# RWKV-7 preparation in a one-layer hybrid encoder: a denser triangular substitution, moved bonus, and moved elementwise work

## The reference, cut to what matters

```python
w_log = -softplus(-(w0 + tanh(w_l) @ w2)) - 0.5
decay = exp(-exp(w_log)); a = sigmoid(a0 + a_l @ a2); g = sigmoid(g_l) @ g2
kk = heads(k * k_k); kk = kk / max(sqrt(sum(kk * kk)), 1e-12)
k = k * (1 + (a - 1) * k_a)
state = state * w + (state @ -kk) (kk * a)^T + v k^T     # token by token
y = state @ r
y = groupnorm(y) * ln_w + ln_b + sum(r * k * r_k) * v    # the bonus
out = y * g
```

## Time and profile before

| what | value |
|---|---|
| median of 3 runs | 1804.3 us (1803.42 to 1804.86) |
| the profiled execution, its own time | 1807.21 us |
| its span, first to last instruction | 1805.4 us |
| PE busy | 1738.3 us (96%) |
| DVE / ACT / POOL busy | 988.2 / 796.3 / 693.3 us |
| mean granted TensorE clock | 0.979 |

### The profile page before, as it was taken

The page is one execution under the profiler, slowest core; times in us unless marked ns, Lnnn a source line. Parts: engine busy times, 40 slices in busy tenths (PEclk is TensorE's granted clock), DMA queues, the critical chain, the costliest instruction groups (busy, mean ns, idle before and its releaser), DMA issues.

```text
span 1805.4 us, 30026 instructions
## 1 busy us (share of the span) xinstructions
PE 1738.3 (96%) x11960; PEld 1321.0 (73%) x11960; DVE 988.2 (55%) x1551; ACT 796.3 (44%) x1519; POOL 693.3 (38%) x502
## 2 busy tenths in 40 slices
PE   7999999999998998999999999999999999999997
PEld 4766666665575766768888768878888888888886
DVE  6543232325464756453340462388856775884788
ACT  5313233235342443541120232467666666756763
POOL 2211202010120111223333103398686876968772
PEclk9999999998989999999999999999999999999999
DMA  5101000000212114051211102202202022030202
GB/s 206 47 24 33 22 35 13 21 5 18 54 20 43 26 40 110 27 205 38 79 47 49 33 0 65 75 25 70 77 29 83 24 70 66 28 93 25 70 1 93
DMA packets 81681, 94.36 MB, mean 52 GB/s; under 512 B 53648, under 2 KB 56208, under 8 KB 81552
## 3 DMA queue, kind: packets, MB, share of 16 engines
q1 hardware_dynamic: 81552, 92.56, 16.7%
HBM read 82.57 MB, written 9.98 MB: 51 GB/s over the span
## 4 chain that ended last, share of the span: by engine, by line
PE 85%; DVE 7%; DMA 3%; ACT 3%; issue 2%; POOL 1%; SPq 1%; DVEq 0%; ACTq 0%; POOLq 0%
PE PS L1652 33%; PE PS L934 16%; PE PS L994 8%; PE PS L1095 3%; PE PS L1113 2%; PE PS L1134 2%; PE PS L1599 2%; PE PS L1168 1%; PE PS L1577 1%; PE PS L1444 1%; PE PS L1459 1%; DMA xt_dram<-sc_s 1%; PE PS L1171 1%; PE PS L1359 1%; PE PS L1302 1%
## 5 line engine op out<-in xcount | busy, mean ns | idle before, releaser
L1652 PE MATMUL PS<-memr,wsp 128*128 128x512 f32 x1332 | 319.9, 391 | 2.4 <-POOL wsp L895 2.4
L934 PE MATMUL PS<-xn,wsp 128*128 128x512 f32 x1344 | 309.1, 391 | 6.7 <-DVE xn L2212 6.7
L934 PEld LDWEIGHTS PS<-xn,wsp 128*128 128x128 f32 x1344 | 252.8, 189 | 62.8 <-DVE xn L2212 5.9
L1652 PEld LDWEIGHTS PS<-memr,wsp 128*128 128x128 f32 x1332 | 249.7, 188 | 57.7 <-POOL wsp L895 3.3
L776 POOL CAST wsp<-wraw 128x1024 fp32r<-128x1024 f32 x40 | 42.7, 1068 | 468.8 <-PE PS L934 302.3
L1652 PE MATMUL PS<-memr,wraw_r 128*128 128x512 f32 x684 | 165.7, 391 | 0.7 <-POOL wraw_r L895 0.7
L994 PE MATMUL PS<-xn,wsp 128*128 128x512 f32 x576 | 149.5, 407 | 3.3 <-DVE proj L2261 3.1
L895 POOL TENSOR_TENSOR wsp<-sa,wsp 128x512 fp32r<-128x512 f32 x86 | 115.2, 1342 | 89.9 <-ACT wsp L2103 89.8
L1652 PEld LDWEIGHTS PS<-memr,wraw_r 128*128 128x128 f32 x684 | 128.2, 188 | 29.1 <-POOL wraw_r L895 1.1
L994 PEld LDWEIGHTS PS<-xn,wsp 128*128 128x128 f32 x576 | 106.4, 192 | 41.4 <-issue 20.7
L1776 ACT ACTIVATE H<-PS,mst 128x128 f32<-128x128 f32 (+3 forms) x64 | 47.5, 743 | 184.9 <-DVE mst L2342 179.7
(11 more groups left out here) (349 smaller groups left out, 3170.3 us busy)
## 6 DMA issues: line engine op xcount, KB each, us to landing
wraw<-in_weights_dram SPq DMA_DIRECT2D x40, 512.0 KB, 3.6
sa<-in_weights_dram SPq DMA_DIRECT2D x32, 512.0 KB, 4.2
H<-in_x_dram SPq DMA_DIRECT2D x16, 512.0 KB, 6.7
sbx<-in_weights_dram SPq DMA_DIRECT2D x32, 256.0 KB, 2.9
sa<-in_weights_dram SPq DMA_DIRECT2D x32, 256.0 KB, 2.8
H<-in_weights_dram SPq DMA_DIRECT2D x8, 512.0 KB, 6.5
out_dram<-sbx SPq DMA_DIRECT2D x16, 256.0 KB, 2.1
a_dram<-H SPq DMA_DIRECT2D x16, 128.0 KB, 2.5
```

The source lines that it names most:

```text
L934: last = nc.tensor.matmul(PS[:, 2 * k + half, :], wsp[:, k, kt, a, :], src[:, at, b, HALF * half:HALF * half + HALF], start=(i == 0 and (a ...
L1652: last = nc.tensor.matmul(PS[:, g % PS_BANKS, :], w[:, a, win(k)], x[:, b, :], start=(k == 0 and (a, b) == (0, 0)), stop=(k == ROWS - 1 an ...
```

## The change

- **Substitution**: steps j = 8 to 14 move from places 29 to 33 to places 28 to 30, `xt` from 33 to 30. The bonus moves from places 31 and 32 to 33 and 34.
- **Moves between engines**: `kk` (the scaled key) goes from VectorE to ScalarE (place 9, a copy with a scale), and ScalarE squares the unscaled key with the scale inside the activation (place 4). `na` goes to ScalarE (place 3). `b` goes to GpSimd (place 13).
- **Order**: `ks0`, `ks1` one place sooner (5, 6); `kf` at 7, `W` and `Wi` at 8; `nkk` at 12, `k2` at 13, `rt` at 14; the `al` products one place sooner (17 to 20); `rk` at 22; memsets at 23. The table for heads 6 and 7 follows.
- **One activation table**: explicit loads of a set that holds both logarithm and exponential, at the start, before the latent norms and at place 6. A dummy logarithm at the start goes.
- **`local`**: the two products with a selection matrix per head (L1359) both use all 128 rows. Before, one of them used 64 rows.
- **Ahead of the loop**: places 0 to 3 of pair 1 run before the doubling of pair 0, not between its steps, on TensorE and VectorE.
- **SyncE**: a wait on `tok` of the pair before is added ahead of one load.

```diff
-SUBST = {26: (0, 1, 2, 3), 27: (4, 5, 6, 7), 29: (8,), 30: (9,), 31: (10, 11), 32: (12, 13), 33: (14,)}
-BONUS = 31
+SUBST = {26: (0, 1, 2, 3), 27: (4, 5, 6, 7), 28: (8, 9, 10, 11), 29: (12, 13), 30: (14,)}
+BONUS = 33
...
-                return ((0,), (1,), (2,), (3, 4), (5, 6), (7, 8, 9), (10, 11), (12, 13, 14), (15, 16, 17))[i]
-            return ((), (18, 19), (20, 21, 22), (24,), (), (26, 27), (29, 30, 31), (32, 33), ())[i - 9]
+                return ((0,), (1,), (2,), (3, 4), (5, 6), (7, 8, 9), (10, 11), (12, 13), (14, 15, 16))[i]
+            return ((), (17, 18), (19, 20), (21, 22, 23), (), (26, 27), (28, 29, 30), (33, 34), ())[i - 9]
...
                 if p < PAIRS - 1:
+                    if p >= 1:
+                        sp.wait_ge(L_PE.sem, L_PE.at(f"tok{p - 1}_{NW - 1}", -1))
                     sp.dma_start(o_places[p], o_dram[p]).then_inc(o_loaded, 16)
...
+                if s == 13:
+                    pool.wait_ge(P_DVE.sem, P_DVE.at(f"nkk_{n}", -1))
+                    nc.gpsimd.tensor_tensor(rA, rA, rKK, ALU.mult).then_inc(P_POOL.sem, P_POOL.one(f"b_{n}"))
...
-                    for c, rows in ((h, chunk(h)), (1 - h, slice(0, P))):
-                        last = nc.tensor.matmul(to_r(c), con[rows, C_SEL + CH * h:C_SEL + CH * h + CH],
-                                                rAR[p % 2][rows, w, 1, chunk(c)], start=False, stop=True)
+                    for c in range(2):
+                        last = nc.tensor.matmul(to_r(c), con[:, C_SEL + CH * h:C_SEL + CH * h + CH],
+                                                rAR[p % 2][:, w, 1, chunk(c)], start=False, stop=True)
...
+            for s in range(4):
+                beside(0, s)
             for lv in range(LEVELS):
                 for w in range(2):
                     double_q(lv, 0, w)
-                beside(0, 2 * lv)
                 for w in range(2):
                     double_z(lv, 0, w)
-                beside(0, 2 * lv + 1)
...
+            nc.scalar.preload_act_table_set("natural_log_exp_and_others")
             for kt in range(KT):
                 act.wait_ge(x_loaded[kt], 16)
...
             act.wait_ge(eps_made, 1)
-            nc.scalar.activation(small[:, 41:42], small[:, 40:41], ACT.Ln)
...
+                if s == 3:
+                    r_at(P_ACT, f"ta1_{n}")
+                    nc.scalar.activation(rA, rA, ACT.Copy, scale=-0.5, bias=-0.5).then_inc(sem_, one("na"))
+                if s == 4:
                     if n >= 2:
                         r_at(L_PE, f"tok{n - 2}_{NW - 1}")
-                    nc.scalar.activation(rBh[i], rKK, ACT.Square).then_inc(sem_, one("kksq"))
+                    nc.scalar.activation(rBh[i], proj[:, T_K + n, :], ACT.Square, scale=vech[:, 8 + n:9 + n]).then_inc(
+                        sem_, one("kksq"))
+                if s == 6:
+                    nc.scalar.preload_act_table_set("natural_log_exp_and_others")
...
-                if s == 33:
+                if s == max(SUBST):
                     own(f"xa{BLK - 2}")
                     r(nc.vector.tensor_copy(bXT, bX.rearrange("p i n -> p n i")), "xt")
```

More of the change, by code:

```diff
@@ L477, in build @@
                                            "rk0", "rk1"]))
-        P_ACT = Steps(sem("prep_act"), each(["tw0", "tw1", "ta0", "ta1", "kksq", "kl0", "kl1", "W", "kf", "Wi", "wt0", "wt1", "afirst"]))
+        P_ACT = Steps(sem("prep_act"), each(["tw0", "tw1", "ta0", "ta1", "na", "kksq", "kl0", "kl1", "kf", "W", "Wi", "kk", "wt0", "wt1", "afirst"]))
         P_DVE = Steps(sem("prep_dve"), each(
[L480 to L483, removed]
+            ["t1p", "L", "am", "nkk", "k2", "at", "bt", "kt", "al0", "al1", "al2", "al3", "rk", "x0", "x1"]
+            + [y for place in SUBST for j in SUBST[place] for y in (f"xm{j}", f"xa{j}")] + ["xt", "bv0", "bv1"]))
+        P_POOL = Steps(sem("prep_pool"), each(["b", "rt", "kh", "bh"]))
         O_PE = Steps(sem("post_pe"), each(["vs0", "vs1", "lg0", "lg1"]))
@@ L1831, in prep @@
                     nc.scalar.activation(rB[i][:, halves(s - 6)], PS[:, 7, :], ACT.Ln).then_inc(sem_, one(f"kl{s - 6}"))
-                if s == 10:
+                if s == 7:
+                    r_at(P_ACT, f"kl1_{n}")
+                    nc.scalar.activation(rB[i], rB[i], ACT.Exp, scale=-0.5).then_inc(sem_, one("kf"))
+                if s == 8:
                     r_at(P_DVE, f"L_{n}")
@@ L1837, in prep @@
                     nc.scalar.activation(rW, rWi, ACT.Exp, scale=-half_e).then_inc(sem_, one("W"))
-                    r_at(P_ACT, f"kl1_{n}")
-                    nc.scalar.activation(rB[i], rB[i], ACT.Exp, scale=-0.5).then_inc(sem_, one("kf"))
-                if s == 11:
                     r_at(P_ACT, f"W_{n}")
                     nc.scalar.activation(rWi, rWi, ACT.Exp, scale=half_e).then_inc(sem_, one("Wi"))
-                if s == 12:
+                if s == 9:
+                    nc.scalar.activation(rKK, proj[:, T_K + n, :], ACT.Copy, scale=vech[:, 8 + n:9 + n]).then_inc(
+                        sem_, one("kk"))
+                if s == 10:
                     if n >= 2:
@@ L2400, in prep @@
                     r(nc.vector.tensor_tensor_scan(rWi, rStep, rT1, 0.0, ALU.mult, ALU.add), "L")
-                if s == 4:
-                    r_at(P_ACT, f"ta1_{n}")
-                    r(nc.vector.tensor_scalar(rA, rA, -0.5, -0.5, ALU.mult, ALU.add), "na")
-                if s == 4:
-                    own("na")
+                if s == 5:
+                    r_at(P_ACT, f"na_{n}")
+                    own("L")
                     r(nc.vector.tensor_scalar(rT1, rA, 1.0, vec[:, V_KA + n:V_KA + n + 1], ALU.add, ALU.mult), "am")
-                if s == 5:
+                if s == 12:
+                    r_at(P_ACT, f"kk_{n}")
+                    r(nc.vector.scalar_tensor_tensor(rKK, rB[i], 1e12, rKK, ALU.min, ALU.mult), "nkk")
+                if s == 13:
                     own("am")
                     r(nc.vector.scalar_tensor_tensor(rT1, rT1, 1.0, kk_, ALU.subtract, ALU.mult, reverse0=True), "k2")
-                if s == 14:
-                    r_at(P_ACT, f"kf_{n}")
-                    r(nc.vector.scalar_tensor_tensor(rKK, rB[i], 1e12, rKK, ALU.min, ALU.mult), "nkk")
                 if s == 15:
@@ L2421, in prep @@
                 if s == 16:
-                    r(nc.vector.tensor_tensor(rA, rA, rKK, ALU.mult), "b")
-                if s == 16:
-                    own("b")
+                    r_at(P_POOL, f"b_{n}")
                     r_at(P_ACT, f"Wi_{n}")
@@ L2429, in prep @@
                     r(nc.vector.tensor_tensor(kk_, rT1, rWi, ALU.mult), "kt")
-                if 18 <= s < 22:
-                    k = s - 18
+                if 17 <= s < 21:
+                    k = s - 17
                     r_at(P_PE, f"al{k}_{n}")
@@ L2440, in prep @@
                         f"al{k}")
-                if s == 21:
+                if s == 22:
                     r_at(P_POOL, f"rt_{n}")
                     r(nc.vector.scalar_tensor_tensor(r_, r_, vec[:, V_RK + n:V_RK + n + 1], rT1, ALU.mult, ALU.mult), "rk")
-                if s == 24:
+                if s == 23:
                     if n >= 1:
@@ L2449, in prep @@
                     r(nc.vector.memset(sc_s[:, 3456:3712:BLK + 1], 1.0), "x1")
-                if s in (BONUS, BONUS + 1):
-                    k = s - BONUS
-                    r_at(P_PE, f"rk{k}_{n}")
-                    if k == 0 and n == 0:
-                        m_at(M_PE, f"qp{MLA_HEADS - 1}")
-                    r(nc.vector.tensor_tensor(rBV[n][:, halves(k)], PS[:, 7, :], v_[:, halves(k)], ALU.mult), f"bv{k}")
                 if s in SUBST:
@@ L2468, in prep @@
                         r(nc.vector.tensor_tensor(below, below, part, ALU.add), f"xa{j}")
-                if s == 33:
+                if s == max(SUBST):
                     own(f"xa{BLK - 2}")
                     r(nc.vector.tensor_copy(bXT, bX.rearrange("p i n -> p n i")), "xt")
+                if s in (BONUS, BONUS + 1):
+                    k = s - BONUS
+                    r_at(P_PE, f"rk{k}_{n}")
+                    if k == 0 and n == 0:
+                        m_at(M_PE, f"qp{MLA_HEADS - 1}")
+                    r(nc.vector.tensor_tensor(rBV[n][:, halves(k)], PS[:, 7, :], v_[:, halves(k)], ALU.mult), f"bv{k}")
             def post(m, s):
```

26 lines of the change are left out of this document (9 added, 17 removed).

## The result

The changed kernel is slower: 1827.0 us median of 4 runs (1823.1 to 1827.7) beside 1803.9 of 4 for the kernel before. The ratio on record is 1.0141, with a 95% interval of 1.0119 to 1.0163; the quotient of the two medians, 1.0128, lies inside it. Two executions in the chip's slow state (2800.65 us of the kernel before, 1938.71 us of the one with five things undone) are in no ratio here. I had predicted 1806, range 1797 to 1812. The profiled execution after took 1823.12 us over a span of 1821.3, 15.9 more than the span of before; the other three spans were 1824.8 to 1825.9.

A forecast was written before the change was run, and what follows sets the result against it. TensorE, busy 96% of the span, was taken as the bound, with room only in the RWKV loop. Gains and costs summed to +1.6 us on an expected median of 1804.3, rounded to 1806 us; range 1797 to 1812.

The forecast's parts named there:

- `b` on GpSimd: In the preparation, b takes 2.4 us on GpSimd and ends before bt reads it: nothing; 0.5 a pair if nkk were late.
- The stalls: TensorE's three waits for inverse matrices from DRAM vanish because xt ends 3.9 us sooner: -7.6 us.
- The clock behind them: After those DRAM waits, the low granted clock costs 2.5, 1.4 and 1.4 us, which come back: -5.3 us.
- The denser order's own waits: In group 2, TensorE waits for VectorE's state copy and scores, partly offset by mt coming sooner: +1.05 us.
- Tables: Activation table loads removed at the start (-1.3 us) and in pair 3 (-0.75 us); nothing in post or the latent norms.
- Head 6: TensorE's 2.25 us standstill before ks0, from late squares on ScalarE, shrinks: -1.7 us (nothing to -3.5).
- `al0` in the gap of `mt`: In group 1, al0 fills TensorE's idle 0.6 us at mt: -0.9 us in all; in head 7, kt's place costs +1.1.
- The selection: In local, two more 128-row records per group cost 0.117 us, 64 times: +7.0 us, bounds 0 to +14.
- End of attention: In head 7, rk1 waits for bv0 and the last transposes start at 479.05; a DMA wait absorbs 0.9: +3.0 us.
- Ahead of the loop: Pair 1's low-rank products, no longer filling pair 0's doubling, have their own waits, with more low clock: +4.8 us.
- The first: Rival: the clock stays up between attention and loop, giving back 9 us: 1797 us; chance 0.27.
- The second: Rival: the wait moves to the end of attention, behind rk0, and lowers the clock there too: 1811 us; chance 0.25.

The follow-up runs named there:

- the one with five things undone: Changed kernel with b and na on VectorE, tanh's set loaded at place 34, rk0 and rk1 in two slots, 64-row selection restored: ratio 0.9981.
- the kernel with the new order added: Kernel before plus the denser substitution and places 0 to 3 of pair 1 ahead of pair 0's doubling: ratio 0.9966.
- the run with the start alone: Kernel before plus the denser substitution and one logarithm-exponential table at the start and ahead of the latent norms: ratio 0.9974.
- the early set: Changed kernel with the activation set that holds tanh loaded at place 34: ratio 1.0082; with b also back on VectorE, 1.0040.
- interleaving: Changed kernel with places 0 to 3 of pair 1 again between the steps of pair 0's doubling: ratio 1.0159.

## Why the prediction was wrong, step by step

Two terms that the sum has at nothing made most of the miss: `b` on GpSimd, and the table that the next tanh finds. Those are the steps that failed.

- **The stalls: right.** All three are gone, and `xt` comes when worked out.
- **The clock behind them (-5.3): right as a mechanism, wrong in the changed kernel.** With the substitution alone the pair changes run at 1.00. In the changed kernel another wait took the stall's place and lowered the clock for longer. The size was taken from one execution, and that one was slow for its kernel: 1807.21 us with a clock of 0.979, where 34 others have 1794.65 to 1807.76 us and a mean of 0.9825. From trace to trace both terms come out: the groups of `xt`'s stalls (group 3 of pairs 0 to 2) take 23.7, 22.7 and 19.3 us before and 18.0, 19.3 and 15.2 with the substitution, 13.2 us for the 12.9 of my two terms. In the mean of all executions the whole edit gives 6.8 us, and the 11.9 that I gave it is outside the interval of 3.2 to 10.4. So the usual execution probably loses less clock behind the stalls than the profiled one did (argued, not shown).
- **The denser order's own waits (+1.05): right place, too small.** TensorE's waits for the state copy from 500 to 735 us are 3.3 us, for 0.6 before, and in the kernel with the new order added group 2 takes 1.2, 0.5 and 0.3 us longer in pairs 0 to 2.
- **Tables: this step failed.** "Nothing" beyond the start and pair 3 counted the loads that go and not the set that is left active. It priced each new load by where the edit puts it, not where the old sets had made one unnecessary. In pair 3 the expected 0.7 us came (a gap of 0.45 for 1.17). At the start, the exponential begins at 18.76 for 21.05, and attention at 401 us is 0.9 ahead of before, not 1.3; the run with the start alone did not repeat the gain.
- **`b` on GpSimd: this step failed most.** "Nothing; were `nkk` 2 us late, 0.5 a pair" took both engines' durations as they are alone; the runs showed that the two wait for each other. Undone in the changed kernel it gives 6 us, and 7.6 beside the early set (1.0082 to 1.0040); done alone in the kernel before it costs 22 (interval 1.0099 to 1.0145).
- **Head 6: half right.** The wait of 2.25 us for the squares is gone, and 0.69 us for the first logarithm stands in its place (up to 4.0 in the experiments' profiles). New waits came: 2.20 us at 426.32, where five activations in a row hold up a softmax, and the 3.02 behind `at` and `bt`. With `b` on VectorE that one is replaced by one of 2.40 for the masks of `al0`, which the moved places cause.
- **`al0` in the gap of `mt`: not seen.** `bt` came too late for it, and TensorE waited 1.0 us ahead of it instead.
- **The selection (+7.0): mechanism right, size somewhat large.** In the traces 12 of the 15 groups that can be compared show 0.46 us, 5.6 in all; in time it was 3.8, within overlapping intervals. The groups that wait for VectorE hide it, which I had allowed for in pair 0 only.
- **`na` (+2.2): right**, 1.09 us in each of two pairs, without its part in the clock.
- **End of attention (+3.0): right for its own part**, `rk1` waits 3.08 us. With `na` it is worth 6.8 instead of 5.2. But the last transposes start at 482.7 us and not at 479.05, since the wait behind `at` and `bt` lies ahead of them.
- **Ahead of the loop (+4.8): wrong.** From the first low-rank product to `solve` it took 14.2 us, for 16.3 predicted, and the low clock there lasted 6.8 us and not 13.7. Two experiments find no loss in it.
- **The rivals.** The first happened in part: more of the stretch ahead of the loop ran at full clock. The second had its wait but not, in the profile of the changed kernel, its low clock; four of the experiments' profiles, such as that of interleaving, have one there (6.8 us at the low level). No rival had the two mechanisms that decided.

Put in order, the steps from 1.0141 are: set for tanh -0.59%, `b` -0.42%, `na` and bonus -0.38%, selection -0.21%; 0.19% remain to 0.9962, for the moved places, `kk` on ScalarE, the tables, the new order ahead of the loop and that of heads 6 and 7. These were not all taken apart. Only the first of these steps has intervals that lie apart from each other; that the others are there rests on the traces beside them.

## What to carry to other kernels

Before work is moved to GpSimd, list what VectorE does in the same microseconds: two SBUF inputs there and a read here exclude each other, and the duration of neither in a quiet stretch is its price. When a table set is replaced, follow the active set to the next function of each kind, over the loop's edge. And price a wait together with the clock behind it: three loads of 1.28 us, with two waits of 1.42, cost some 10.6.

## What the runs showed of the hardware that I had not expected

- The turns of VectorE and GpSimd: `bt` 4.49 us for 1.23 alone, behind two GpSimd instructions in a row, so the waiting one can lose the next turn as well; `b` 3.37 for 2.35.
- A table load ahead of an activation is not taken while the engine idles: it stands behind the activation's wait (7.22 us idle, then 1.28 of load). With the set loaded at place 34, no tanh has a load ahead.
- The granted clock turns small edits into larger ones and hides others. A 1.42 us wait was followed by 10.2 us at the lower level, and three waits of 3.2 us by 6.8, 6.8 and 13.6. Work taken from TensorE (the selection) brought no time in the changed kernel; whether the clock took it is argued, not shown.
